# Forgetting attention in a two-layer trunk: two heads' scores as three products on 64-row tiles, exponentials one step later

## The reference, cut to what matters

```
q, k, v, f_logit = jnp.split(proj, [HD, 2 * HD, 3 * HD], axis=-1)
cum = jnp.cumsum(jax.nn.log_sigmoid(f_logit + f_bias), axis=1)
...
s = jnp.einsum('bqhd,bkhd->bhqk', qb, k) * scale
s = s + cb[..., None] - cum_k[:, :, None, :]
s = jnp.where((k_pos[None, :] <= q_pos[:, None])[None, None], s, NEG_INF)
p = jax.nn.softmax(s, axis=-1)
return jnp.einsum('bhqk,bkhd->bqhd', p.astype(v.dtype), v)
```

## Time and profile before

| | |
|---|---|
| median of 3 runs | 2323.47 us (2323.45 to 2328.69) |
| profiled execution, its own time | 2331.4 us |
| its span, first to last instruction | 2329.6 us |
| busy: TensorE | 2255.2 us, 97% |
| busy: VectorE, ScalarE, GpSimd | 1198.5, 854.2, 567.6 us |
| granted TensorE clock | 0.988 of full speed on average |
| forgetting attention | 1311.9 us (first product) to about 1538 us |

### The profile page before, as it was taken

The page is one execution under the profiler, slowest core; times in us unless marked ns, Lnnn a source line. Parts: engine busy times, 40 slices in busy tenths (PEclk is TensorE's granted clock), DMA queues, the critical chain, the costliest instruction groups (busy, mean ns, idle before and its releaser), DMA issues.

```text
span 2329.6 us, 32539 instructions
## 1 busy us (share of the span) xinstructions
PE 2255.2 (97%) x11512; PEld 1839.1 (79%) x11512; DVE 1198.5 (51%) x1885; ACT 854.2 (37%) x1526; POOL 567.6 (24%) x423
## 2 busy tenths in 40 slices
PE   7998898999999999999999999999899999999998
PEld 6876686888888788877888777778688888878887
DVE  5659568444444434337332476646844444443432
ACT  3127334333333312222221477733433333331223
POOL 2423332222232000110000366643222222200011
PEclk9999998999999999999999999999999999999999
DMA  7340441322221613223442877544122222162312
GB/s 230 98 105 2 154 154 33 96 87 82 81 81 63 246 56 131 90 74 117 145 153 99 219 178 179 138 153 146 37 90 87 87 88 81 63 230 72 131 48 79
DMA packets 253241, 261.20 MB, mean 112 GB/s; under 512 B 15968, under 2 KB 221024, under 8 KB 248176
## 3 DMA queue, kind: packets, MB, share of 16 engines
q1 hardware_dynamic: 242160, 220.32, 31.8%
q10 hardware_dynamic: 11008, 39.92, 4.4%
HBM read 187.92 MB, written 65.08 MB: 109 GB/s over the span
## 4 chain that ended last, share of the span: by engine, by line
PE 89%; DVE 6%; DMA 2%; ACT 1%; POOL 1%; issue 1%; SPq 0%; ACTq 0%; DVEq 0%
PE psum L1713 12%; PE psum L1714 12%; PE psum L1715 12%; PE psum L1983 11%; PE psum L1985 11%; PE psum L1987 11%; PE psum L1861 3%; PE psum L1886 3%; PE psum L1961 2%; PE psum L1963 2%; PE psum L1962 2%; PE psum L1821 1%; PE psum L1822 1%; DVE b_full L1453 1%; DVE set_lo L1472 1%; DVE b_lo L1438 1%
## 5 line engine op out<-in xcount | busy, mean ns | idle before, releaser
L1983 PE MATMUL psum<-b_hi,a_hi 128*128 128x512 f32 x1232 | 484.6, 393 | 20.6 <-DVE b_lo L1438 20.6
L1987 PE MATMUL psum<-b_hi,a_lo 128*128 128x512 f32 x1232 | 482.7, 392 | 0.0
L1985 PE MATMUL psum<-b_lo,a_hi 128*128 128x512 f32 x1232 | 482.6, 392 | 0.0
L1983 PEld LDWEIGHTS psum<-b_hi,a_hi 128*128 128x128 f32 x1232 | 233.4, 189 | 72.5 <-issue 24.1
L1713 PE MATMUL psum<-set_hi,dw_hi 128*128 128x512 f32 x704 | 274.8, 390 | 3.2 <-DVE set_lo L1472 3.2
L1714 PE MATMUL psum<-set_lo,dw_hi 128*128 128x512 f32 x704 | 273.9, 389 | 0.0
L1715 PE MATMUL psum<-set_hi,dw_lo 128*128 128x512 f32 x704 | 273.9, 389 | 0.0
L1985 PEld LDWEIGHTS psum<-b_lo,a_hi 128*128 128x128 f32 x1232 | 233.5, 190 | 48.6 <-issue 0.5
L1987 PEld LDWEIGHTS psum<-b_hi,a_lo 128*128 128x128 f32 x1232 | 233.3, 189 | 49.0
L782 POOL TENSOR_TENSOR a_sum<-a_raw 128x512 f32<-128x512 f32 x88 | 114.6, 1302 | 501.2 <-DVE a_lo L1433 442.7
L748 POOL TENSOR_TENSOR score<-score,inv_l 128x128 f32<-128x128 f32 (+7 forms) x128 | 144.9, 1147 | 355.6 <-DVE inv_l L1319 353.9
(11 more groups left out here) (205 smaller groups left out, 3604.0 us busy)
## 6 DMA issues: line engine op xcount, KB each, us to landing
a_raw<-in_ffn_w_gate_up SPq DMA_DIRECT2D x88, 512.0 KB, 5.1
hid_scr<-hid_out SPq DMA_DIRECT2D x44, 512.0 KB, 5.7
set_full<-hid_scr SPq DMA_DIRECT2D x22, 1024.0 KB, 6.2
x_t<-x_scr SPq DMA_DIRECT2D x16, 1024.0 KB, 8.3
dw_raw<-in_ffn_w_down SPq DMA_DIRECT2D x32, 512.0 KB, 3.8
x_scr<-x_t ACTq DMA_DIRECT2D x24, 512.0 KB, 2.6
w_raw<-in_fox_w_in SPq DMA_DIRECT2D x22, 512.0 KB, 4.0
w_raw<-in_swa_w_out SPq DMA_DIRECT2D x16, 512.0 KB, 4.1
```

Of the source, the lines that this page charges most:

```text
L1983: T.matmul(out_ps, a_hi[i][:, j, :], b_hi[i][:, j, :], start=not more and j == 0, stop=False, skip_group_check=True)
L1985: T.matmul(out_ps, a_hi[i][:, j, :], b_lo[i][:, j, :], start=False, stop=False, skip_group_check=True)
L1987: last = T.matmul(out_ps, a_lo[i][:, j, :], b_hi[i][:, j, :], start=False, stop=j == KH - 1, skip_group_check=True)
```

## The change

- The operands lie differently. A pair's four tensors `q_hi`, `q_lo`, `k_hi`, `k_lo` hold head 0 in rows 0 to 63 and head 1 in rows 64 to 127. SyncE loads a pair's heads with 4 transfers of 512 KB instead of 12 of 256 KB.
- A step's scores of both heads are made together: for each chunk of columns three products (high x high, high x low of the keys, low of the queries x high), each as two matmuls with a contraction over 64 rows, on the row tiles `rows(0)` and `rows(1)`. Low x low is left out. The causal product stays a matmul on the whole array, one for each head.
- `qk` does nothing at places of head 0 and both heads at places of head 1. Its wait, with the count `n` of head 1, is now for the scores of both heads of the step before.
- `ahead` is 6 for products and scores (three steps), 4 for the rest. VectorE takes the scores of both heads one after the other at places of head 1.
- The rows of `cum` have two sets of buffers and are loaded with the heads.

```
-                self.ahead = dict(qk=4, scores=4, exps=3, inverse=3, norm=3) if self.fox else \
+                self.ahead = dict(qk=6, scores=6, exps=4, inverse=4, norm=4) if self.fox else \
...
             def load_heads(a, u, b):
                 wait(sp, a.max_done, 2 * a.steps * (u - 1))
+                q_hi, q_lo, k_hi, k_lo = fox_operands(u, b)
+                for part, q, k in ((0, q_hi, k_hi), (1, q_lo, k_lo)):
+                    sp.dma_start(q[:, :].bitcast(FP32), fox_qk[part][bass.ds(u * P, P), :]).then_inc(a.qk_in[b], 16)
+                    sp.dma_start(k[:, :].bitcast(FP32), fox_qk[part][bass.ds(FOX_H * HD + u * P, P), :])\
+                        .then_inc(a.qk_in[b], 16)
                 for e in range(2):
...
+                    sp.dma_start(fox_cum(u, e, b)[:, :], cum_scr[bass.ds(2 * u + e, 1), :].to_broadcast([P, SEQ]))\
+                        .then_inc(a.qk_in[b], 16)
...
+            def score_pair(a, pi, i, last, b):
+                if ahead := a_step(a, pi, i, last):
+                    scores(a, *ahead, (b if i < 2 * a.steps else 1 - b))
+                    scores(a, *a_step(a, pi, i + 1, last), (b if i < 2 * a.steps else 1 - b))
...
             def qk(a, u, e, s, b=0):
                 n = a.count(u, e, s)
-                at0 = e * SEQ
+                if a.fox and not e:
+                    return
 
                 wait(pe, a.max_done if a.fox else a.exp_done, n - (1 if a.fox else 3))
...
                             diagonal = cc + ww == w
-                            T.matmul(ps, q_hi[:, qs], key[:, cc:cc + ww], start=True, stop=False)
-                            last = T.matmul(ps, q_lo[:, qs], key[:, cc:cc + ww], start=False,
-                                            stop=not diagonal)
+                            for q, k in ((q_hi, k_hi), (q_hi, k_lo), (q_lo, k_hi)):
+                                for r in range(2):
+                                    T.matmul(psum[:, r * SEQ + at1:r * SEQ + at1 + ww], q[rows(r), qs], k[rows(r), cc:cc + ww],
+                                             start=q is q_hi and k is k_hi, stop=q is q_lo and not diagonal)
                             if diagonal:
-                                last = T.matmul(ps[:, ww - P:ww], ident_bf[:, :], causal_bf[:, :], start=False,
-                                                stop=True)
+                                for r in range(2):
+                                    last = T.matmul(psum[:, r * SEQ + at1 + ww - P:r * SEQ + at1 + ww], ident_bf[:, :],
+                                                    causal_bf[:, :], start=False, stop=True)
+                                    if t == a.tiles[s][-1]:
+                                        last.then_inc(a.qk_done, 1)
```

More of the change, by code:

```diff
@@ L63, in trunk @@
         swa_crossed = [at(f"swa_crossed{i}", 52 + 4 * i, [P, TT, P]) for i in range(2)]
[L65 to L69, removed]
+        fox_loads = [[at(f"fox_{w}_{n}", k, [P, SEQ], F32R) for w, k in zip(("q_hi", "q_lo", "k_hi", "k_lo"), ks)]
+                     for n, ks in (("even", (120, 124, 128, 132)), ("odd", (64, 68, 72, 76)), ("first", (142, 146, 150, 158)))]
+        fox_v_in = [at(f"fox_v{b}", (136, 48)[b], [P, TT, P]) for b in range(2)]
         swa_q = at("swa_q", 0, [P, SWA_Q // 2, SEQ])
@@ L484, in fox_operands, with fox_cum @@
             return fox_loads[2 if isinstance(u, int) and u == 0 else b]
[L486 to L492, removed]
+        def fox_cum(u, e, b):
+            return cum_first if isinstance(u, int) and u == 0 and e == 0 else cum_all[b][e]
         w_in_view = {"swa": swa_w_in[0].rearrange("(k p) n -> p k n", p=P),
@@ L526, in load_heads @@
                 wait(sp, a.max_done, 2 * a.steps * (u - 1))
-                for e in range(2):
[L528 to L542, removed]
+                q_hi, q_lo, k_hi, k_lo = fox_operands(u, b)
[3 more added lines that the diff above has]
+                        .then_inc(a.qk_in[b], 16)
+                for e in range(2):
+                    sp.dma_start(fox_cum(u, e, b)[:, :], cum_scr[bass.ds(2 * u + e, 1), :].to_broadcast([P, SEQ]))\
+                        .then_inc(a.qk_in[b], 16)
             def load_v(a, u, b):
                 wait(sp, a.pv_done, a.groups * (u - 1))
-                sp.dma_start(fox_v_of(b)[:, :, :], fox_v[bass.ds(u * P, P), :, :]).then_inc(a.v_in[b], 16)
+                sp.dma_start(fox_v_in[b][:, :, :], fox_v[bass.ds(u * P, P), :, :]).then_inc(a.v_in[b], 16)
             def swap_halves(c):
@@ L1358, in pair_dve @@
                     probs_copy(a, u, e, s)
[L1359 removed]
+                    if a.fox:
+                        if e:
+                            score_pair(a, pi, i + a.ahead["scores"] - 1, last, b)
+                        if ahead := a_step(a, pi, i + a.ahead["inverse"], last):
+                            inverse(a, *ahead)
+                    elif ahead := a_step(a, pi, i + a.ahead["scores"], last):
                         scores(a, *ahead)
[L1361 to L1362 removed]
                     if done := a_done(a, pi, i, first):
@@ L1369, in attention @@
                 late = a.ahead["scores"] - a.ahead["inverse"]
-                for i in range(a.ahead["scores"]):
-                    if a.fox or i >= SWA_EARLY:
-                        scores(a, *a_step(a, 0, i, False))
-                    if i >= late:
-                        inverse(a, *a_step(a, 0, i - late, False))
+                if a.fox:
+                    for i in range(0, a.ahead["scores"], 2):
+                        score_pair(a, 0, i, False, 0)
+                        for j in range(max(i - late, 0), i + 2 - late):
+                            inverse(a, *a_step(a, 0, j, False))
+                else:
+                    for i in range(a.ahead["scores"]):
+                        if i >= SWA_EARLY:
+                            scores(a, *a_step(a, 0, i, False))
+                        if i >= late:
+                            inverse(a, *a_step(a, 0, i - late, False))
                 pair_dve(a, 0, True, False)
@@ L1881, in pv @@
                 if a.fox:
[L1882 removed]
+                    v = fox_v_in[b]
                     for k in range(t + 1):
```

31 lines of the change are left out of this document (13 added, 18 removed).

## The result

| | before | after |
|---|---|---|
| median of 4 runs each, measured side by side | 2326.08 us | 2359.95 us |
| profiled execution, its own time | 2331.4 us | 2364.65 us |
| its span | 2329.6 us | 2362.8 us |
| first product of the forgetting attention | 1311.92 us | 1315.12 us |
| from there to its last value product | 225.87 us | 255.20 us |

The changed kernel takes 1.0142 times as long, with a 95% interval of 1.0111 to 1.0173. Slower was forecast, but +14 us, and it is +34 us; 2359.95 lies 2 us above the range. The stage itself gives +29.3 us. Another 3.2 lie ahead of its first product, where of the change only the transfers of the first pairs run.

A forecast was written before the change was run, and what follows sets the result against it. TensorE's stream alone was taken to bound the forgetting attention. Stream -3, added waits +14 and start +3 gave +14 us, a median of about 2337 (2330 to 2344), with a range over rivals of 2321 to 2358 us.

The forecast's parts named there:

- The products: TensorE's score products: three for two heads side by side on row tiles, 6.7 us a pair for 8.96, saving 2.2.
- loads in turn: Rival: the two row tiles load their weights one after the other, +18 us, 2355 us; chance 0.10.
- tiles that don't overlap: Rival: the row tiles run one after the other, 6.7 us more per pair, +54 us, 2391 us; chance 0.05.
- The switches: TensorE changing between whole array and tiles: 0.18 us going in, 0.09 going out; 3.7 us a pair against 2.4 before.
- cover: TensorE's work between two steps' products, transposes and value products, that runs while VectorE drains both heads' scores.
- The drain after step 5: Before the next pair's step 0: drain 2.82 us, cover of 12 transposes 1.53, so TensorE stands still 1.3 us.
- The drain after step 1: Before step 2's products: drain 2.70 us, cover of 16 transposes 1.96, so TensorE waits 0.7 us.
- VectorE's wait for the rows of `cum`: On VectorE, 16.7 us before the change: it goes away, and TensorE had no share in it.
- The start: First three steps in a row with nothing between: 10.7 us from first product to step 1's transposes, 7.9 before; +3 us.
- The added depth and the loads: Work on ScalarE and GpSimd 4 places ahead instead of 3, and SyncE's loads a pair ahead: counted as nothing.
- Free switches: Rival: tile mode changes cost nothing, the stream gives back 2.0 us more per pair, 2321 us, no change; chance 0.12.
- faster: Rival: free switches and a drain the transposes cover; 2312 us with half of the waits gone too; chance 0.05.

The follow-up runs named there:

- turns: Changed kernel with a pair's last transpose fills ordered so that each takes a PSUM bank used three fills before; 2346.4 us, ratio 1.0071.
- split_fill: turns with value products moved between the steps, a pair's last group split around the next pair's step 3, and unread products at the start; 2338.19 us, ratio 1.0025.
- twice5: turns plus a second reading by VectorE of head 1's scores at step 5 of each pair; 2374.31 us, ratio 1.0186.
- turns_before: The kernel before with the bank order of turns, as a control; 2328.7 us, ratio 0.9989.
- depth: The kernel before with only the changed one's depth: products and scores 6 places ahead, exponentials, reciprocals and normalization 4; 2328.96 us, ratio 0.9996.
- products: The changed kernel with the old depth: products and scores 4 places ahead, exponentials, reciprocals and normalization 3; 2360.59 us, ratio 1.0121.
- fill: The changed kernel plus 13 unread products over 512 columns in TensorE's waits of the first steps; 2359.66 us, ratio 1.0132.
- turns_fill: turns plus the 13 unread products of fill in the waits of the first steps; 2344.83 us, ratio 1.0072.
- twice2: turns plus a second reading by VectorE of head 1's scores at step 2 of each pair; 2348.11 us, ratio 1.0072.

## Why the prediction was right in direction and wrong in size

**The products: right.** Side by side on row tiles, 6.7 us a pair for 8.96. The records of a pair of tiles start some 3 ns apart, and their two weight loads last 0.19 us together, as long as one, so loads in turn and tiles that don't overlap are both out.

**The switches: right in kind.** Going in, the products start 0.07 before the end of the transposes (1367.82, 1367.75), as forecast; their first pair takes 0.33 (1367.75, 1368.08), where the first product before took 0.31, and the last one before the mask takes 0.33 as well (1369.01, 1369.34), where it took 0.24 (1357.61, 1357.85). The stream of a pair can be had by taking drain minus cover off the pair, as the prediction defines them: in the changed kernel 30.05 - (2.88 - 1.53) - (3.94 - 1.96) = 26.7, in `turns` 28.8 - (2.89 - 1.53) - (2.70 - 1.96) = 26.7. That is 0.3 less than before, where 0.4 was forecast. This is an estimate, and `split_fill` sets a limit to it: with hardly a wait of the matmuls left it has 27.5. 0.4 of the 0.8 between them are the ten transposes above, mostly the wait for their bank, and it has one more group of value products, with its ways in and out; the rest I can't place. Either way nearly all of the 2.2 us that the products save is paid back. Had the switches been free, the stream would be near 25. The Trainium skill (TensorEngine Tiling (Array Packing), Key Properties) has the array drain at each change of mode. The trace fits that: the next product starts 0.07 us before the end of the last record, where it starts 0.25 before it without a change.

**The drain after step 5: right.** 2.88 for 2.82, a wait of 1.35 for 1.3. `twice5` shows that this place has no slack.

**The drain after step 1: the step that failed.** The prediction took the cover of 16 transposes at its length, 1.96, and a wait of 0.7 us. It named the copies only as waiting for the transposes ("for those wait ScalarE's and VectorE's copies"). That a transpose in its turn waits for the copy that frees its bank it left out, and so put at nothing without a reason. The bank of the last four is freed by a copy that stands in VectorE's queue behind both heads' scores, so the cover could not run during the drain that it was to cover. The wait was 3.94 - 1.96 = 2.0 instead of 0.7, seven times: +9 us. `turns` takes just this away and finds the forecast's 2.70. `turns_before` shows that the line costs little without the scores side by side, and the traces say that the depth alone doesn't do it: TensorE's waits for VectorE's copies are 0.5 us over the stage in `depth`, 6.7 in `products`, which has the scores side by side at the old depth, and 13.7 with both.

The line that moves the last bank stood in the kernel before as well, and its trace had the sign. Three times, 1.9 us in all, TensorE waited before the same four transposes for the same copy. In two of the three VectorE's scores ahead of the copy had been held by the row of `cum`; this is the first of them:

```profile
1339.05 0.29 DVE L1295 CUSTOM_DVE_ANT_0 score<-psum,cum_all 128x128 f32<-128x128 f32 x1 [1.46 <-DMA cum_all<-cum_scr]
...
1339.69 0.67 DVE L1335 COPY fox_p<-psum 128x512 f32<-128x512 f32 x1
...
1340.41 0.66 PE L1861 MATMUL psum<-ident,score 128*128 128x128 f32 x4 [0.55 <-DVE fox_p L1335]
```

So TensorE did have a share in VectorE's wait for the rows of `cum`, small though it is, where the prediction gave it none. Whatever stands ahead of that copy on VectorE holds TensorE.

**The last pair: the same fault.** After its step 5, where the prediction had no wait, TensorE waits 1.4 us for a bank (1556.03), again for a copy of VectorE. It stands in `turns` as well (1.39), and in `twice5`, where one more read of step 5's scores is ahead of the copy, it is 2.75.

**The start: too low, by the clock and by a group left out.** Forecast 10.7 us from the first product to the transposes of step 1, measured 14.55 (1315.12 to 1329.67). `fill`, at full clock, has 12.6, so 2.0 are the clock. The other 1.9 are the products of step 3. With the deeper order they stand ahead of those transposes, and the forecast has no term for them; in `fill` it is 2.0 from their start to the transposes (1320.18, 1322.17), a wait of 0.4 for GpSimd included. The products are work brought forward, not added. What the clock does is shown by the products after the waits:

```profile
1318.01 0.66 PE L1819 MATMUL psum<-fox_k_hi_first,fox_q_hi_first 64*128 64x384 f32 x2 [1.34 <-DVE neg_max L1276]
...
1320.58 0.63 PE L1819 MATMUL psum<-fox_k_hi_first,fox_q_lo_first 64*128 64x512 f32 x2
1321.14 0.40 PE L1823 MATMUL psum<-causal_bf,ident_bf 128*128 128x128 bf16 x2
1323.90 0.50 PE L1819 MATMUL psum<-fox_k_hi_first,fox_q_hi_first 64*128 64x512 f32 x2 [2.36 <-DVE neg_max L1276]
1324.24 0.39 PE L1819 MATMUL psum<-fox_k_lo_first,fox_q_hi_first 64*128 64x512 f32 x2
```

After 1.34 us without work a product over 512 columns lasts 0.63, at 1324.24 again 0.39, and from 1324.9 on it is half clock once more. The whole first pair is 27.04, against 20.72 before; the forecast's terms make 20.72 + 2.8 + 1.3 - 0.4 = 24.4, and `fill`, with the start at full clock, has 24.26. That these two agree so well is in part luck, since in `depth` the deeper order alone took 2.2 us off the first pair and put 1.7 on the last one. The waits were foreseen, their effect on the clock wasn't: +2.6 us here, and 2 x 1.6 = 3.2 us in later pairs.

**The sum.** On the profiled executions 2331.4 + 14 = 2345.4 was forecast and 2364.65 measured, 19.2 more: 9.0 for the bank, 1.4 in the last pair, 2.6 in the first, 3.2 for two pairs at half clock, 8 x 0.14 = 1.1 for the stream, 3.2 ahead of the stage, 0.7 behind it; less 1.7, since three pairs of before were themselves 0.3 to 0.8 us longer than 26.96 by the waits shown above. Together 19.5. How the parts divide between the first and the last pair is an estimate. The 3.2 ahead of the stage have no cause shown. The added depth and the loads cost nothing, as counted.

**The rivals.** Free switches, faster, loads in turn and no overlap: each is against a measured number. The loads in turn come nearest to the measured total, with 2355, but by luck, as their mechanism isn't there. The range failed because it took its upper end from that rival and gave the waits only 0.3 us; no case had a wait of another kind behind the one that was added.

## What to carry to other kernels

When both halves of a double buffer are drained together, don't only ask whether the work queued behind is long enough to cover the drain: ask of each piece of that cover which buffer it takes, who frees that, and whether the freeing instruction stands behind the drain on the same engine. A short wait of that kind in the profile of the kernel before, though it costs next to nothing there, names the place. Saving work on the engine that is the bound can be worth nothing if it puts in waits of a us or two; here they cost their length, and sometimes the clock of what followed. Before packing the array, count the changes of tile mode that it brings: here 0.18 us for each way in and 0.10 for each way out took back nearly all of a saving of 25% on the products.

## What the runs showed of the hardware

- Two row tiles of 64 rows run wholly side by side on these float32 parts, which are multiplied in one pass: 0.23 to 0.24 us for a pair of products over 512 columns, the time of one product on the whole array. At 128 columns a pair of products takes 0.11 (1384.57 to 1384.67).
- Waits of 1.0 and 1.8 us in a pair of 30 us can be enough for 3.4 us at half clock: two later pairs fell in the changed kernel, four in `fill`, and with waits of 2.3 and 0.6 (`twice5`) all seven. With waits of 1.0 and 0.6 none fell in `turns` and one each in `turns_fill` and `twice2`. In `products` TensorE was as idle, in pieces of at most 1.5 us, and none fell. So it isn't the idle share alone; what else decides is open.
- Taking away waits at one place can move the half clock to a later one and leave the total as it was (`fill`: first pair 2.8 us shorter, two more pairs at half clock). Each of these is seen in one trace of its kernel.
